# Dilated attention in a transformer kernel: turning two rounds behind the scores, output chunks begun over six tiles, scaling on VectorE

## What is computed

```python
def _dilated_attention(h, w_q, q_gain, w_o, k_pads, v_pads, rel_bias):
    q = (h @ w_q).reshape(bsz, seq, B_GROUPS, B_HEADS, B_HEAD_DIM)      # 3 groups, 16 heads of 64
    q = _rms(q, q_gain[:, None, :]) * (B_HEAD_DIM ** -0.5)
    ...
            s = jnp.einsum('birhd,bjrhd->bhrij', qb, kb).astype(f32) + biases[g][None, :, None]
            s = jnp.where(valid[None, None], s, -jnp.inf)
            lse = jax.nn.logsumexp(s, axis=-1)
            p = jnp.exp(s - lse[..., None]).astype(vb.dtype)
            o = jnp.einsum('bhrij,bjrhd->birhd', p, vb)
    ...
        wts = jax.nn.softmax(jnp.stack(lses), axis=0)
        o = jnp.einsum('gbqh,gbqhd->bqhd', wts, jnp.stack(outs))
    return o @ w_o
```

## Time and profile before

| | |
|---|---|
| median of three runs | 2185.96 us |
| profiled execution | 2191.01 us |
| its span | 2189.2 us |
| mean granted TensorE clock | 0.949 of 2.4 GHz |
| TensorE busy | 2011.5 us, 92% |
| VectorE busy | 1163.3 us, 53% |
| ScalarE busy | 991.6 us, 45% |
| GpSimd busy | 506.5 us, 23% |

### The profile page before, as it was taken

How to read it: one execution, slowest core, us unless ns; L and a number is a source line. 1 busy time by engine, 2 the same in 40 slices (tenths; PEclk the granted TensorE clock), 3 DMA queues, 4 the chain that set the end, 5 groups by cost and what they waited for, 6 DMA issues and landing times.

```text
span 2189.2 us, 36847 instructions
## 1 busy us (share of the span) xinstructions
PE 2011.5 (92%) x15863; PEld 1925.3 (88%) x15863; DVE 1163.3 (53%) x1356; ACT 991.6 (45%) x1157; POOL 506.5 (23%) x142
## 2 busy tenths in 40 slices
PE   7887999989999989999887999999999988869999
PEld 6875899988899979999886999999899977649998
DVE  5336577665577764337784643433444355536443
ACT  4325444355443453336334443476643455625433
POOL 1100122322022221320340123333222312121322
PEclk9867999999899999999998999999999999979999
DMA  7300345443245525555321455445455554314552
GB/s 261 136 18 1 116 155 195 166 162 135 97 144 198 194 98 192 172 182 183 125 79 56 156 189 176 160 163 169 152 182 189 177 166 141 105 61 148 179 186 102
DMA packets 57314, 321.13 MB, mean 147 GB/s; under 512 B 5694, under 2 KB 19125, under 8 KB 19829
## 3 DMA queue, kind: packets, MB, share of 16 engines
q1 hardware_dynamic: 55444, 313.93, 41.5%
q10 hardware_dynamic: 1760, 5.63, 0.7%
HBM read 318.41 MB, written 1.12 MB: 146 GB/s over the span
## 4 chain that ended last, share of the span: by engine, by line
PE 72%; DVE 12%; issue 7%; ACT 5%; POOL 2%; DMA 2%; SPq 0%; ACTq 0%; DVEq 0%; POOLq 0%
PE bank L371 22%; PE bank L372 21%; PE bank L373 21%; DVE lo L344 3%; ACT hi L338 1%; PE bank L430 1%; DVE xl L839 1%; DVE arena L519 1%; PE bank L1512 1%; POOL lo L344 1%; ACT arena L1673 1%; DMA arena<-rel_rows 1%; POOL arena L501 1%; DVE arena L1587 1%; PE bank L1067 1%
## 5 line engine op out<-in xcount | busy, mean ns | idle before, releaser
L371 PE MATMUL bank<-xh,hi 128*128 128x256 f32 x3208 | 923.6, 288 | 37.1 <-DVE xl L839 20.2
L372 PE MATMUL bank<-xl,hi 128*128 128x256 f32 x3208 | 916.5, 286 | 0.0
L373 PE MATMUL bank<-xh,lo 128*128 128x256 f32 x3208 | 916.1, 286 | 0.0
L338 ACT ACTIVATE hi<-ring 128x2048 fp32r<-128x2048 f32 x291 | 550.5, 1899 | 476.6 <-PE bank L373 471.1
L344 POOL TENSOR_TENSOR lo<-ring,hi 128x2048 fp32r<-128x2048 f32 x90 | 421.1, 4680 | 1409.4 <-ACT hi L338 1409.4
L344 DVE TENSOR_TENSOR lo<-ring,hi 128x2048 fp32r<-128x2048 f32 x201 | 524.4, 2610 | 384.5 <-ACT hi L338 384.3
L371 PEld LDWEIGHTS bank<-xh,hi 128*128 128x128 f32 x3208 | 624.1, 195 | 49.9 <-issue 32.8
L372 PEld LDWEIGHTS bank<-xl,hi 128*128 128x128 f32 x3208 | 624.2, 195 | 0.6 <-issue 0.5
L373 PEld LDWEIGHTS bank<-xh,lo 128*128 128x128 f32 x3208 | 623.9, 194 | 0.2
L371 PE MATMUL bank<-gh,hi 128*128 128x256 f32 x1056 | 302.3, 286 | 16.7 <-DVE gl L775 15.9
L372 PE MATMUL bank<-gl,hi 128*128 128x256 f32 x1056 | 301.1, 285 | 0.0
(11 more groups left out here) (263 smaller groups left out, 1857.6 us busy)
## 6 DMA issues: line engine op xcount, KB each, us to landing
ring<-in_ffn_in SPq DMA_DIRECT2D x132, 1024.0 KB, 4.9
ring<-in_ffn_out SPq DMA_DIRECT2D x66, 1024.0 KB, 4.9
ring<-in_kv SPq DMA_DIRECT2D x24, 1024.0 KB, 4.8
ring<-in_hg_in SPq DMA_DIRECT2D x16, 1024.0 KB, 4.9
ring<-in_od_in SPq DMA_DIRECT2D x12, 1024.0 KB, 5.0
ring<-in_dq SPq DMA_DIRECT2D x12, 1024.0 KB, 4.9
ring<-in_ev_in SPq DMA_DIRECT2D x11, 1024.0 KB, 4.9
arena<-rel_rows SPq DMA_DIRECT2D x16, 384.0 KB, 5.6
```

What stands on the lines that cost most here:

```text
L338: nc.scalar.activation(hi[n % RING][:, 0:words[n]], ring[n % RING][:, 0:words[n]], ACT.Copy).then_inc(hi_ok, 1)
L371: nc.tensor.matmul(out_, lh, rh, start=start, stop=False, **kw)
L372: nc.tensor.matmul(out_, lh, rl, start=False, stop=False, **kw)
L373: return nc.tensor.matmul(out_, ll, rh, start=False, stop=stop, **kw)
```

## The change

In the block "dilated" alone: turning and values run two rounds behind the scores instead of one, group by group in every round, so there is a tenth round, 9. The inserted projection keeps its place between scores and turning of group 2. A mask of group g now waits for the turning of the same group two units before, not for that whole unit. GpSimd's scaling loop is gone: VectorE scales the weights of unit i-1 in round i, between its masks and its maxima. GpSimd gets the split of every odd chunk, where it had chunks 1 and 3. The first masks come before `take_out` of chunk 4. In ScalarE's rounds with an inserted projection, exponentials come before the last group's turned weights. Outputs go to banks 0 to 3 instead of 4 to 7. Chunks 12 and 13 are begun after round 8 over six of the eight tiles of K, chunk 14 over six within round 9 for its first half. Four places of bias loads on SyncE's queue move up by one chunk (10, 11, 13 and 14 become 9, 10, 12 and 13). The diff has one line of context around each edit.

```diff
--- before.py
+++ after.py
@@ -306,7 +306,7 @@
             elif b == "dilated":
-                lo_by += ["P" if c in (1, 3) else "V" for c in range(len(streams[b]))]
+                lo_by += ["P" if c % 2 else "V" for c in range(len(streams[b]))]
             elif b == "hgrn":
@@ -379,12 +379,16 @@
         class Soft:
-            def __init__(self, units, ns, late, att, pt, nm, rr, copies, held=(), by_pool=False):
-                self.by_pool = by_pool
+            def __init__(self, units, ns, late, att, pt, nm, rr, copies, held=(), woven=False):
+                self.woven = woven
                 self.units, self.ns, self.late, self.att, self.pt, self.nm, self.rr = units, ns, late, att, pt, nm, rr
                 self.nr = len(att)
+                self.filled = set()
                 self.before = {"pe": {}, "dve": {}, "act": {}}
@@ -480,9 +484,9 @@
                         s.step[i, g](pe)
-                    if i >= s.lag and i not in s.exps_first:
+                    if i >= s.lag and (i not in s.exps_first or s.woven):
                         turn(i - s.lag, g)
-                if i >= s.lag and i in s.exps_first:
+                if i >= s.lag and i in s.exps_first and not s.woven:
                     for g in range(ns):
@@ -493,21 +497,13 @@
-        def soft_pool(pool, s):
-            for u in range(len(s.units)):
-                pool.wait_ge(*s.at("rec", u + 1))
-                for e in range(2):
-                    for out, exps, r in scaled(s, u, e):
-                        last = nc.gpsimd.tensor_tensor(out, exps, r, ALU.mult)
-                    last.then_inc(soft_sem["p"], 1)
-
         def soft_dve(dve, s):
                 un = s.units[i]
-                if i >= s.nr:
+                if i >= s.nr and not s.woven:
                     dve.wait_ge(*s.at("turned", 2 * ns * (i - s.nr + 1)))
@@ -515,9 +511,13 @@
                     dve.wait_ge(*s.at("qk", w + 1))
+                    if i >= s.nr and s.woven:
+                        dve.wait_ge(*s.at("turned", 2 * (w - s.nr * ns) + 2))
                     for e in range(2):
                                                 ALU.add).then_inc(soft_sem["masked"], 1)
+                if s.woven and i >= 1:
+                    weights(i - 1)
                 for e in range(2):
@@ -537,11 +537,10 @@
                     rec_step(nc.vector.tensor_tensor(both[:, :, 2:4], both[:, :, 2:4], un["gate"], ALU.mult))
-                if not s.by_pool:
-                    for e in range(2):
-                        for out, exps, r in scaled(s, u, e):
-                            last = nc.vector.tensor_tensor(out, exps, r, ALU.mult)
-                        last.then_inc(soft_sem["p"], 1)
+                for e in range(2):
+                    for out, exps, r in scaled(s, u, e):
+                        last = nc.vector.tensor_tensor(out, exps, r, ALU.mult)
+                    last.then_inc(soft_sem["p"], 1)
@@ -564,7 +563,7 @@
                 s.hook(s.mid, "dve", i, dve)
-                if s.late and i >= 1:
+                if s.late and i >= 1 and (not s.woven or i == U):
                     weights(i - 1)
@@ -582,16 +581,16 @@
-            def exps(u):
-                for e in range(2):
+            def exps(u, heads=(0, 1)):
+                for e in heads:
                     act.wait_ge(*s.at("max", 2 * u + e + 1))
-            def turned(j):
-                for g in range(ns):
+            def turned(j, parts=None):
+                for g in range(ns) if parts is None else parts:
                     w = j * ns + g
@@ -602,6 +601,20 @@
                 u, j = (i - 1 if s.late else i), i - s.lag
+                if s.woven:
+                    early = ns - 1 if i in s.filled else ns
+                    if j >= 0:
+                        turned(j, range(early))
+                    if i < U:
+                        exps(i)
+                    if j >= 0:
+                        turned(j, range(early, ns))
+                    s.hook(s.mid, "act", i, act)
+                    if j >= 1:
+                        pair_out(j - 1)
+                    s.hook(s.after, "act", i, act)
+                    continue
                 if i in s.exps_first and 0 <= u < U:
@@ -658,6 +671,21 @@
                 pe_half(pe, n, B, mode, h, width, first, tiles)
+        def pe_part_of(pe, n, B, h, ks, tiles):
+            if h == 0 and 0 in ks:
+                wait_split(pe, n)
+                nc.tensor.matmul(B[:, :], zero16[:, :], zero16[:, :].unsqueeze(1).broadcast_to([1, 4, P]), start=True,
+                                 stop=False, skip_group_check=True)
+            wh, wl = slot(n, CW, hi), slot(n, CW, lo)
+            e = slice(h * P, (h + 1) * P)
+            for k in ks:
+                tiles(k)
+                last = product(B[:, h * T:(h + 1) * T], wh[:, k, e], wl[:, k, e], xh[:, k, :], xl[:, k, :],
+                               False, k == KT - 1, skip_group_check=True)
+            if h == 1 and KT - 1 in ks:
+                last.then_inc(chunk_mul, 1)
@@ -845,7 +873,7 @@
                     dve.wait_ge(y_bank if kind == "y" else chunk_mul, val)
-                    y = bank[4 + i][:, :].rearrange("p (e t) -> p e t", e=2)
+                    y = y_bank_of(b, i)[:, :].rearrange("p (e t) -> p e t", e=2)
                     if scale is None:
@@ -906,6 +934,10 @@
             dve.wait_ge(rs_new, st)
+        def y_bank_of(b, i):
+            return bank[i if before.get(b) == "dilated" else 4 + i]
@@ -1922,7 +1954,7 @@
             N_HELD = 2
-            soft = Soft(units, 3, False, att, pt, NM, RR, copies, [DK[:, p, :] for p in range(N_HELD)], True)
+            soft = Soft(units, 3, True, att, pt, NM, RR, copies, [DK[:, p, :] for p in range(N_HELD)], True)
@@ -1947,7 +1979,7 @@
                 if hg >= 2:
-                    pe.wait_ge(*soft.at("pt", 12 * (hg - 1)))
+                    pe.wait_ge(*soft.at("pt", 12 * (hg - 1) - 6))
                 for g in order:
@@ -1955,7 +1987,7 @@
                     if h == 0 and c >= 5:
-                        pe.wait_ge(lin, c)
+                        pe.wait_ge(lin, c if c > 5 else 4)
                         if c in (6, 9):
@@ -2012,7 +2044,7 @@
-                return {4: [0], 10: [1], 11: [2], 13: [3], 14: [4], 15: [5, 6, 7]}.get(c, [])
+                return {4: [0], 9: [1], 10: [2], 12: [3], 13: [4], 15: [5, 6, 7]}.get(c, [])
@@ -2022,6 +2054,8 @@
                         norms(dve, normed[i - 1])
+                    if i == 0:
+                        take_out(dve, 4)
                     if i in inside:
@@ -2039,18 +2073,47 @@
-            soft.turn_after = {j: (log_ok, 3 * hg + 3) for j, hg in normed.items()}
-            soft.step = {(i, 2): lambda pe, c=c: project(pe, c) for i, c in inside.items()}
+            def out_ready(pe):
+                return lambda k: pe.wait_ge(*soft.at("o", k + 1)) if k >= N_HELD else pe.wait_ge(held_l, 1)
+            def out_first(pe):
+                pe.wait_ge(*soft.at("masked", 48))
+                for c in (0, 1):
+                    for h in range(2):
+                        pe_part_of(pe, n0 + 12 + c, bank[c], h, range(6), out_ready(pe))
+            def out_third(ks):
+                def run(pe):
+                    pe_part_of(pe, n0 + 14, bank[2], 0, ks, out_ready(pe))
+                return run
+            def out_rest(pe):
+                for k in (6, 7):
+                    for c in (0, 1):
+                        for h in range(2):
+                            pe_part_of(pe, n0 + 12 + c, bank[c], h, (k,), out_ready(pe))
+                pe_part_of(pe, n0 + 14, bank[2], 0, (6, 7), out_ready(pe))
+                pe_part_of(pe, n0 + 14, bank[2], 1, range(8), out_ready(pe))
+                pe_half(pe, n0 + 15, bank[3], "fm", 0)
+                pe_half(pe, n0 + 15, bank[3], "fm", 1)
+            soft.turn_after = {max(j - 1, 0): (log_ok, 3 * hg + 3) for j, hg in normed.items()}
+            soft.filled = set(inside)
+            soft.step = ({(i, 2): lambda pe, c=c: project(pe, c) for i, c in inside.items()}
+                         | {(9, 1): out_third(range(3)), (9, 2): out_third(range(3, 6))})
             soft.after["pe"] = ({i: lambda pe, c=c: project(pe, c) for i, c in behind.items()}
-                                | {i: lambda pe, hg=hg: means(pe, hg) for i, hg in normed.items()})
+                                | {i: lambda pe, hg=hg: means(pe, hg) for i, hg in normed.items()} | {8: out_first})
             soft.mid["dve"] = {i: dve_mid(i) for i in range(6)}
             soft.mid["act"] = {i: lambda act, c=c: squares(act, c) for i, c in inside.items()}
+            soft.mid["act"][0] = lambda act: (squares(act, 4), squares(act, 5))
             soft.after["act"] = ({i: lambda act, c=c: squares(act, c) for i, c in behind.items()}
             soft.before["act"] = {6: held_high}
-            soft.exps_first = set(inside)
@@ -2062,8 +2125,7 @@
                 soft_pe(pe, soft)
```

(9 more changed lines are left out.)

## The result

The changed kernel takes 2220.65 us, the median of four runs (2217.35 to 2222.44); the kernel before, run beside it, 2187.89 (2180.75 to 2193.05). The ratio is 1.015, with a 95% interval of 1.0117 to 1.0183: slower by 33 us. Forecast were 2225 and a range of 2199 to 2241. The profiled execution of the changed kernel took 2217.35 us.

A forecast was written before the change was run, and what follows sets the result against it. The prediction took TensorE as almost full in rounds 2 to 4, with gains possible only in the last rounds. Terms -0.3 + 34.4 - 2.0 + 6.3 = +38.4 us on the 2186.0 median gave 2224.4, stated as 2225; range 2199 to 2241.

The forecast's parts named there:

- The chain: Rounds 2 to 5: VectorE's and ScalarE's work after group 2's turning is exposed; TensorE stands still 35.0 us in all.
- The clock: Rounds 2 to 4: after each standstill TensorE runs at the low clock; granted clock falls from 1.00 to about 0.8.
- Rounds 0 and 1: Stage start: earlier scores, but round 1's second projection waits until 1834 and runs at the low clock; -0.3 us.
- Rounds 2 to 5: Middle rounds: standstills and low clock make them 28.9, 31.8, 28.6 and 16.6 us long; +34.4 us.
- Rounds 6 and 7: Scaling leaves the path, but bias transfer and masks impose 17.5 us a pair; 31.7 against 33.7 us, -2.0.
- Rounds 8, 9 and outputs: Stage end: TensorE waits for ScalarE's exponentials and GpSimd's last split; 45.8 against 39.5 us, +6.3.
- Rival B: Rounds 2 to 5: the chain hides, and GpSimd's 19.5 us is won in the tail; -11 us, 2175; chance 0.09.
- Rival D: VectorE is the bound and slows beside GpSimd, scaling 3.3, splits 3.7 us; 2233; chance within the forecast's 0.58.

The follow-up runs named there:

- kernel 1: The changed kernel with the turning of group 2 before the inserted projection in rounds 2, 3 and 4; 2196.99 us, ratio 1.0050 to the kernel before.
- kernel 2: The changed kernel with VectorE's scaling put behind the maxima, norms and copy instead of before the maxima; 2204.25 us, ratio 1.0086 to the kernel before.
- kernel 4: The changed kernel with all splits as before (GpSimd only chunks 1 and 3, VectorE the others); 2220.41 us, ratio 1.0150 to the kernel before.
- kernel 9: Kernel 6 with output chunks 12 and 13 in three pieces, and VectorE's norms before its maxima in rounds 1, 3 and 5; 2176.28 us, ratio 0.9950.
- kernel 3: The changed kernel with only the last chunk's split (chunk 15) back on VectorE; 2220.00 us, ratio 1.0150 to the kernel before.
- Kernel 6: The changed kernel with group 2's turning before the inserted projection, scaling behind the copy and the last split on VectorE; 2186.44 us, ratio 0.9985.
- kernel 5: The changed kernel with splits as before and the scaling back on GpSimd; 2210.40 us, ratio 1.0095 to the kernel before.
- kernel 10: The kernel before with only the scaling moved to VectorE, at its old place behind the copy; 2182.99 us, ratio 0.9974.

## Why the prediction was right

By its own steps, in the profiled executions:

- *The chain.* Forecast 10.3, 9.4, 10.0 and 8.8 us from the last turning of rounds 2 to 5 to TensorE's next work. The standstills were forecast at 9.4, 8.6, 9.1 and 7.9; the trace has 9.4, 8.5, 9.0 and 7.9. Scaling was taken from two smaller shapes as 3.0; it took 2.77 and a reciprocal of 0.17. The experiments change this chain piece by piece: kernel 1 starts it 5.9 to 6.0 us earlier, kernel 2 takes the scaling out (2.9 us a round), kernel 4 puts a split in (2.2 in round 3) and kernel 9 takes the maxima out (2.6 in round 5).
- *The clock.* That each of these standstills costs the 2.4 GHz level was right; 0.82 to 0.83 in rounds 2 to 4, forecast "about 0.8". The means took 5.4 us as forecast (1862.16 to 1867.5); the second projection of round 3 took 8.0 against 8.8, so this term was 0.8 too large. Round 6 came back to the full level within 4 us (1.00 from 1946.0).
- *Rounds 0 and 1.* Forecast -0.3, measured -3.1 (43.0 against 46.1 from the first scores). Round 1's last mask ended at 1820.2 instead of 1823, as its scores ran at the full clock (0.92 us each, where two took 1.45 and 1.65 before), and its second projection began at 1830.6 instead of 1834.
- *Rounds 2 to 5.* Forecast +34.4, measured +31.4. Each round came out 0.3 to 1.2 us shorter than forecast.
- *Rounds 6 and 7.* Forecast -2.0, measured -5.9 (27.8 against 33.7). This is the term that was most off. I took 9 us from a bias's issue to its mask, and 8.5 for the masks. The rows are

```profile
1951.53 2.96 SPq L2043 DMA_DIRECT2D arena<-rel_rows  x4
...
1959.19 0.42 DVE L555 TENSOR_TENSOR xl<-bank,xh 128x256 fp32r<-128x256 f32 x1 [2.15 <-ACT xh L582]
1959.53 1.01 DVE L517 TENSOR_TENSOR arena<-bank,arena 128x384 f32<-128x384 f32 x2
```

which is 8.0 from issue to mask. By the trace this mask did not wait for the bias: VectorE had stood still for ScalarE (L582, behind its exponentials) and went on without a wait. In kernel 3, the same code but for the last split, it did wait 1.1 us for the bias, from an issue at 1946.44 to the mask at 1955.65, which is 9.2 us. So the two executions differ by at least 1.2 us in this transfer, and that this one took under 9 is chance. Round 7's masks took 8.7 us, as forecast. Round 6's took 6.2 (1945.28 to 1951.50), as TensorE waited for nothing and had the full clock from 1946.0; this is the larger part of the miss.
- *Rounds 8, 9 and outputs.* Forecast +6.3, measured +4.5 (44.0 against 39.5). The wait for ScalarE's exponentials (3.8 us) and for the last split (2.4 us) are both there at the forecast length.

The sum was +38.4 against 26.9 in the block, where the stage was to end 39 us later and ended 26.3 later; the medians moved by 33. All four terms were forecast too large, so the mechanism was right and its sum 11.5 us too high. That 2220.65 lies so near 2225 is in part luck: 6 of the 33 us are scatter of the medians. With the block's 26.9 alone the time would be about 2213, still in the range. Rival B (faster) asked that the chain be hidden behind the projection. Kernel 6 makes just that true for rounds 2 to 4 and has a gain of the kind that B named, only smaller: 4.3 us in the block against 11. Rival D (engines in each other's way) happens in the changed kernel only where it costs nothing. Of GpSimd's five splits from 1796 on, three fell where VectorE was idle and one beside a mask pair. The last met a split on VectorE:

```profile
2003.19 4.57 POOL L344 TENSOR_TENSOR lo<-ring,hi 128x2048 fp32r<-128x2048 f32 x1 [97.28 <-ACT hi L338]
...
2004.95 4.96 DVE L344 TENSOR_TENSOR lo<-ring,hi 128x2048 fp32r<-128x2048 f32 x1 [2.40 <-ACT hi L338]
```

VectorE's took 4.96 us instead of 2.29, but the block's last addition, behind it, waited for TensorE and not for VectorE.

The Trainium skill's rule that both engines contend when VectorE has two SBUF inputs ("GPSIMD Engine Reference", section 8) is borne out by kernel 5 (3.22 us for a split instead of 2.29) and by the row of 4.96 us above: a split has two inputs in SBUF. Its section 4.1 (elementwise work belongs on VectorE) is borne out by kernel 10 and by the durations: 2.77 us for the four scalings on VectorE against 4.46 on GpSimd. That is a factor of 1.6, where the page gives about 2.

## What to carry to other kernels

A new wait is priced by what stands ahead of it on the queue that has to fulfil it, and by all that is queued behind the waiting instruction: here one call on the wrong side of another (turning after the inserted projection) cost 22 us. Move work to a free engine only behind its last answer that somebody waits for; VectorE's scaling cost 2.9 us a round ahead of the maxima and, in the kernel before, gained 7.4 us in all behind the copy. When several edits are bundled, try each alone: early outputs and the scaling on VectorE gained, and the turning two rounds behind, in the order it had, hid them.

## What the runs showed of the hardware

A row of one kernel's trace carried over to another's order within 0.1 us where each engine worked alone, but not where VectorE and GpSimd worked side by side. A split on VectorE took 2.29 us alone and 3.22 beside GpSimd's scaling; the norms took 2.07 and 3.51; GpSimd's four scalings 4.46 alone and 6.51 beside the split. Maxima and mask pairs kept their length (0.94 and 0.54 us; 1.02). I had priced the slower split as a rival, and neither the norms nor GpSimd's own loss.

A split on one engine did not run beside a split on the other. In the trace of the kernel before, twenty splits on VectorE begin during one on GpSimd, the second row among them. Each ends 2.14 to 2.16 us after GpSimd's, however large the overlap. The row of 4.96 us above does the same (2009.91 against 2007.76). Eight splits on GpSimd begin during one on VectorE, and each ends 4.43 to 4.49 us after VectorE's. The split that began first kept its length. So, as the rows have it, the later engine waited for the earlier one's instruction to end and then took about its usual 2.3 or 4.6 us. The price of such a meeting here is what was left of the other engine's instruction, 0.5 to 2.7 us for VectorE, and not a fixed factor.
